# Layer 0's state space in chunks of four tokens, with one scan over 64 chunks

## The reference, cut to what matters

```
# S5_WIDTH 512 = 32 groups of 16 channels, 64 complex states per group, L = 256
def s5_mixer(u, lam_re, lam_im, log_dt, b_re, b_im, c_re, c_im, d_skip, w_glu, b_glu):
    uf = u.reshape(bsz, L, S5_GROUPS, S5_GROUP)
    lam_bar = exp(lam * dt)
    b_bar = ((lam_bar - 1.0) / lam)[..., None] * bmat
    bu = complex(einsum('gnp,blgp->blgn', b_bar.real, uf), einsum('gnp,blgp->blgn', b_bar.imag, uf))
    hstate[t] = lam_bar * hstate[t - 1] + bu[t]            # an associative scan over the 256 tokens
    y = (einsum('gpn,blgn->blgp', c_re, hstate.real) - einsum('gpn,blgn->blgp', c_im, hstate.imag)
         + d_skip * uf)
    y = gelu(y)
    return y * sigmoid(y @ w_glu + b_glu)
```

## Time and profile before

| | before |
|---|---|
| median of 3 runs | 1175.95 us (1174.27 to 1177.32) |
| the profiled execution, its own time | 1179.43 us |
| its span, first to last instruction | 1177.5 us |
| TensorE / VectorE / ScalarE / GpSimd busy | 1063.6 / 793.3 / 506.6 / 371.3 us |
| mean granted TensorE clock | 0.953 of full speed |
| VectorE's first instruction / GpSimd's first after its loads | at 7.9 / 21.9 us |
| end of layer 0's last product | about 296.6 us |

### The profile page before, as it was taken

How to read it: one execution, slowest core, us unless ns; L and a number is a source line. 1 busy time by engine, 2 the same in 40 slices (tenths; PEclk the granted TensorE clock), 3 DMA queues, 4 the chain that set the end, 5 groups by cost and what they waited for, 6 DMA issues and landing times.

```text
span 1177.5 us, 15099 instructions
## 1 busy us (share of the span) xinstructions
PE 1063.6 (90%) x5902; PEld 906.1 (77%) x5902; DVE 793.3 (67%) x1217; ACT 506.6 (43%) x692; POOL 371.3 (32%) x386
## 2 busy tenths in 40 slices
PE   6699898959789897899999997997999999999994
PEld 5466565638688687898888986886998888998883
DVE  5799999976776588444555767666544455767664
ACT  6244235323553343444554332443444555434452
POOL 3715365670372607073442675000000000320001
PEclk9799899888889898999999998998999999999997
DMA  7343232236765476577656664553666545563641
GB/s 257 95 121 94 72 106 91 90 117 206 225 206 171 128 230 210 179 236 217 192 145 210 210 203 143 180 182 104 181 183 192 167 119 160 168 174 110 211 162 54
DMA packets 95047, 191.36 MB, mean 163 GB/s; under 512 B 6800, under 2 KB 10128, under 8 KB 94976
## 3 DMA queue, kind: packets, MB, share of 16 engines
q1 hardware_dynamic: 87408, 166.81, 46.4%
q0 software_dynamic: 6416, 20.88, 5.9%
q10 hardware_dynamic: 1152, 2.71, 0.6%
HBM read 189.32 MB, written 1.05 MB: 162 GB/s over the span
## 4 chain that ended last, share of the span: by engine, by line
PE 67%; DVE 23%; ACT 3%; POOL 3%; issue 3%; DMA 1%; DVEq 0%; SPq 0%; POOLq 0%; ACTq 0%
PE G L557 12%; PE G L559 12%; PE G L558 12%; PE G L566 7%; PE G L569 6%; PE G L568 6%; DVE WL L1359 6%; DVE AR L1638 1%; ACT WH L989 1%; DVE AR L1640 1%; PE B L520 1%; DMA RAW<-in_even_w_in 1%; DVE AR L1621 1%; DVE AR L1620 1%; DVE AR L1459 1%
## 5 line engine op out<-in xcount | busy, mean ns | idle before, releaser
L1359 DVE TENSOR_TENSOR WL<-RAW,WH 128x1024 fp32r<-128x1024 f32 (+2 forms) x306 | 398.0, 1303 | 272.5 <-ACT WH L989 271.6
L989 ACT ACTIVATE WH<-RAW 128x1024 fp32r<-128x1024 f32 (+2 forms) x306 | 319.6, 1047 | 353.6 <-PE G L559 228.9
L557 PE MATMUL G<-WH,HTh 128*128 128x512 f32 (+2 forms) x624 | 257.5, 413 | 20.1 <-DVE WL L1359 19.9
L559 PE MATMUL G<-WL,HTh 128*128 128x512 f32 (+2 forms) x624 | 246.3, 395 | 0.0
L558 PE MATMUL G<-WH,HTl 128*128 128x512 f32 (+2 forms) x624 | 246.0, 394 | 0.0
L566 PE MATMUL G<-HTh,WH 128*128 128x256 f32 x736 | 213.1, 290 | 12.9 <-DVE WL L1359 7.5
L569 PE MATMUL G<-HTh,WL 128*128 128x256 f32 x736 | 211.2, 287 | 0.0
L568 PE MATMUL G<-HTl,WH 128*128 128x256 f32 x736 | 211.2, 287 | 0.0
L557 PEld LDWEIGHTS G<-WH,HTh 128*128 128x128 f32 x624 | 121.1, 194 | 52.8 <-issue 17.7
L566 PEld LDWEIGHTS G<-HTh,WH 128*128 128x128 f32 x736 | 144.3, 196 | 15.3 <-DVE WL L1359 9.3
L568 PEld LDWEIGHTS G<-HTl,WH 128*128 128x128 f32 x736 | 144.2, 196 | 0.1
(11 more groups left out here) (325 smaller groups left out, 1391.8 us busy)
## 6 DMA issues: line engine op xcount, KB each, us to landing
RAW<-in_w_in SPq DMA_DIRECT2D x176, 512.0 KB, 3.8
RAW<-in_even_w_in SPq DMA_DIRECT2D x40, 512.0 KB, 3.6
AR<-in_w_ada POOLq DMA_DIRECT2D x72, 256.0 KB, 3.3
RAW<-in_odd_w_in SPq DMA_DIRECT2D x16, 512.0 KB, 4.4
RAW<-in_w_proj_ret SPq DMA_DIRECT2D x16, 512.0 KB, 4.5
RAW<-in_w_out SPq DMA_DIRECT2D x16, 512.0 KB, 3.5
RAW<-in_even_w_out SPq DMA_DIRECT2D x12, 512.0 KB, 3.6
AR<-in_w_ada SPq DMA_DIRECT2D x24, 256.0 KB, 4.5
```

The source lines that it names most:

```text
L557: nc.tensor.matmul(o, xh, wh, start=begins, stop=False)
L559: ins = nc.tensor.matmul(o, xh, wl, start=False, stop=ends)
L989: return nc.scalar.activation(out_, ps, ACT.Copy, **kw)
L1359: vt(wl, raw, wh.bitcast(F32), ALU.subtract).then_inc(*dve.mark(LO, n))
```

## The change

The tokens of layer 0's state space are taken in chunks of four. Inside a chunk the output is one product with a matrix of 128 by 128 (`NEAR`, with the skip D in it); across chunks the state after each chunk is needed only, so that there are 64 positions to scan and not 256. The states' inputs are one product per tile over four tokens at once (`M2`, the matrix B times powers of lambda, 128 by 128), the outputs one product for four tokens (`M3`, C times powers of lambda). The input `u` is first laid out by chunk (`U4`).

These matrices are made on the chip at the start: powers of lambda and the products with C by VectorE (`s5_powers`, `s5_states_out`), the products with B by GpSimd (`s5_states_in`, six instructions 768 wide), their copies into block form by ScalarE (`s5_block`), `NEAR` by 33 small matmuls and ten copies, `M2` by 32 transposes and eight copies, `U4` by 16 copies. The tables are half as long and made by VectorE alone, in steps 17 to 21 and 25. The scan is two instructions, 1024 wide, over all 16 tiles at once, in steps 43 and 44. The gelu moves from step 87 to steps 60 to 66. The weight pieces and all other layers keep their order.

```diff
-AT_S5_IN = (20, 24, 28, 32, 36, 40, 44, 48, 52, 55, 59, 63, 67, 70, 73, 76)
-AT_S5_SCAN = (26, 30, 34, 38, 42, 46, 50, 54, 57, 61, 65, 69, 72, 75, 78, 82)
-AT_S5_OUT = (33, 37, 41, 45, 49, 53, 56, 60, 64, 68, 71, 74, 77, 81, 83, 84)
-AT_S5_H = (29,) + AT_S5_OUT[:15]
+AT_S5 = {"powers": 1, "factor": 5, "c": 7, "out_re": 9, "out_im": 13, "table": {17: 0, 18: 1, 19: 2, 20: 3, 21: 4, 25: 5},
+         "block": {2: "b0", 8: "cp", 11: "re", 14: "hre", 15: "im", 16: "him"}, "spread": (17, 18, 19, 20), "near": 21,
+         "near_out": (22, 23), "turn": (24, 25, 26, 27), "in": (29, 31, 37, 40), "scan": (43, 44),
+         "back": (45, 48, 51, 54), "out": (49, 52, 55, 58)}
...
-AT_GELU = 87
+AT_GELU = {"square": 60, "cube": 61, "tanh": 63, "y": 64, "hi": 65, "lo": 66}
...
+            def s5_near():
+                ps = take(("near",), S5_NEAR.of("k"))
+                pe.wait_ge(*S5_P.of("dd"))
+                nc.tensor.matmul(ps[:, :], IDENT[0:32, :], DD.rearrange("p a b -> p (a b)"), start=True, stop=False,
+                                 skip_group_check=True)
+                pe.wait_ge(*S5_BLOCK.of("him"))
+                for i in range(16):
+                    for r in range(2):
+                        ins = nc.tensor.matmul(ps[:, 32 * i:32 * i + 32], H[:, r, i, :], CP[:, r, i, :], start=False,
+                                               stop=i == 15 and r == 1, skip_group_check=True)
+                ins.then_inc(*told("near"))
+            def s5_turn(q):
+                for r in range(2):
+                    ps = take(("m2", q, r), S5_M2.of(q, r))
+                    for j in range(4):
+                        ins = nc.tensor.transpose(ps[:, 128 * j:128 * j + 128], H[:, r, 4 * q + j, :], IDENT)
+                    ins.then_inc(*told("m2", q, r))
+            def s5_in(q):
+                ps = take(("s5in", q), S5_IN.of("a2", q))
+                pe.wait_ge(*S5_U4.of("u"))
+                pe.wait_ge(*S5_M2.of(q, 1))
+                for r in range(2):
+                    for j in range(4):
+                        c = 256 * r + 64 * j
+                        ins = nc.tensor.matmul(ps[:, c:c + 64], M2[q][:, r, j, :], U4[:, 4 * q + j, :], start=True,
+                                               stop=True)
+                ins.then_inc(*told("s5in", q))
+            def s5_out(q):
+                ps = take(("s5y", q), S5_Y.of(q))
+                pe.wait_ge(*S5_NEAR.of("k"))
+                pe.wait_ge(*S5_H.of(q))
+                for j in range(4):
+                    o, i = ps[:, 64 * j:64 * j + 64], 4 * q + j
+                    nc.tensor.matmul(o, M3[:, 0, i, :], SH[:, q % 2, 0, j, :], start=True, stop=False)
+                    nc.tensor.matmul(o, M3[:, 1, i, :], SH[:, q % 2, 1, j, :], start=False, stop=False)
+                    ins = nc.tensor.matmul(o, NEAR[:, i, :], U4[:, i, :], start=False, stop=True)
+                ins.then_inc(*told("s5y", q))
...
+            def s5_block(what):
+                for r in range(2):
+                    for g in range(2):
+                        pr, k = slice(64 * g, 64 * g + 64), slice(16 * g, 16 * g + 16)
+                        h = H[pr, r, :, :].rearrange("p i (b k) -> p b i k", b=4)
+                        if what == "b0":
+                            act.wait_ge(l_br, 16)
+                            act.wait_ge(*S5_P.of("zero"))
+                            ins = copy(h[:, 0, :, k], BR[pr, r, :, :])
+                        elif what == "cp":
+                            act.wait_ge(*S5_V.of("cd"))
+                            ins = copy(CP[pr, r, :, k], CD[pr, r, :, :])
+                        elif r == (what in ("im", "him")):
+                            if what in ("hre", "him"):
+                                act.wait_ge(*S5_P.of(what[1:]))
+                                dense = (HA if what == "hre" else HD)[pr, :]
+                                ins = copy(h[:, 1:4, :, k], dense.rearrange("p (b i k) -> p b i k", b=3, i=16))
+                            else:
+                                act.wait_ge(*S5_V.of("zero"))
+                                act.wait_ge(*S5_V.of(what))
+                                o = M3[pr, r, :, :].rearrange("p i (t k) -> p t i k", t=4)
+                                dense = (OA_ if what == "re" else OC_)[pr, :]
+                                ins = copy(o[:, :, :, k], dense.rearrange("p (t i k) -> p t i k", t=4, i=16))
+                ins.then_inc(*act.mark(S5_BLOCK, what))
...
+            def s5_spread(b):
+                act.wait_ge(*GA.of("u", 1))
+                act.wait_ge(*S5_P.of("im"))
+                act.wait_ge(*S5_BLOCK.of("him"))
+                for q in range(4):
+                    u = UT[32 * q:32 * q + 32, :, :].rearrange("p j (c t) -> p j t c", t=4)
+                    ins = copy(U4[32 * b:32 * b + 32, 4 * q:4 * q + 4, :], u[:, :, 3 - b, :])
+                if b == 3:
+                    ins.then_inc(*act.mark(S5_U4, "u"))
...
+            def s5_y(q):
+                act.wait_ge(*side("s5y", q))
+                for tk in range(4):
+                    y = UT[32 * q:32 * q + 32, :, :].rearrange("p j (c t) -> p j t c", t=4)
+                    ps = bank_of["s5y", q][32 * tk:32 * tk + 32, 0:256].rearrange("p (j c) -> p j c", j=4)
+                    ins = copy(y[:, :, tk, :], ps)
...
+            def s5_states_out(part):
+                def product(o, r, p):
+                    c = CD[:, r].unsqueeze(1).to_broadcast([P, 4, 16, 16])
+                    l = LP[:, p, :, :].unsqueeze(3).to_broadcast([P, 4, 16, 16])
+                    vt(o.rearrange("p (t i k) -> p t i k", t=4, i=16), c, l, ALU.mult).then_inc(*dve.tick())
+                if part == "re":
+                    dve.wait_ge(*S5_V.of("cd"))
+                    product(OA_, 0, 0)
+                    product(OB_, 1, 1)
+                    dve.wait_ge(*dve.prev)
...
+                ps = bank_of["s5in", q][:, :].rearrange("p (r n) -> p r n", r=2)
+                tc, tsn = (flat(x[:, 4 * q:4 * q + 4, :]).unsqueeze(1).to_broadcast([P, 2, 256]) for x in (TC, TS))
+                vt(SA.rearrange("p (r n) -> p r n", r=2), ps, tc, ALU.mult).then_inc(*dve.mark(S5_IN, "a1", q))
+                vt(SB_.rearrange("p (r n) -> p r n", r=2), ps, tsn, ALU.mult).then_inc(*dve.mark(S5_IN, "a2", q))
+                c = slice(256 * q, 256 * q + 256)
+                dve.wait_ge(*S5_IN.of("a2", q))
+                vt(V[:, 0, c], SA[:, 0:256], SB_[:, 256:512], ALU.add).then_inc(*dve.mark(S5_IN, "c1", q))
+                vt(V[:, 1, c], SA[:, 256:512], SB_[:, 0:256], ALU.subtract).then_inc(*dve.mark(S5_IN, "c2", q))
+            def s5_scan(r):
+                dve.wait_ge(*S5_IN.of("c2", 3))
+                dve.wait_ge(*S5_P.of("decay"))
+                nc.vector.tensor_tensor_scan(V[:, r, :], flat(DECAY), V[:, r, :], 0.0, ALU.mult, ALU.add).then_inc(
+                    *dve.mark(S5_G, r))
...
+            def s5_states_in():
+                def product(o, r, p):
+                    b = BR[:, r].unsqueeze(1).to_broadcast([P, 3, 16, 16])
+                    l = LP[:, p, 0:3, :].unsqueeze(3).to_broadcast([P, 3, 16, 16])
+                    own()
+                    gtt(o.rearrange("p (d i k) -> p d i k", d=3, i=16), b, l, ALU.mult).then_inc(*pool.tick())
+                pool.wait_ge(l_br, 16)
+                pool.wait_ge(*S5_V.of("lp"))
+                product(HA, 0, 0)
+                product(HB, 1, 1)
                 own()
...
+                gtt(HA, HA, HB, ALU.subtract).then_inc(*pool.mark(S5_P, "re"))
+                product(HB, 0, 1)
+                product(HD, 1, 0)
                 own()
...
+                gtt(HD, HD, HB, ALU.add).then_inc(*pool.mark(S5_P, "im"))
...
+            def s5_back(q):
+                pool.wait_ge(*S5_G.of(1))
+                if q == 0:
+                    own()
+                    nc.gpsimd.memset(SASB.rearrange("p (a c) -> p a c", c=64)[:, :, 0:1], 0.0).then_inc(
+                        *pool.mark(S5_P, "sh"))
+                g = V[:, :, 256 * q:256 * q + 256]
+                tc, tsn = (flat(x[:, 4 * q:4 * q + 4, :]).unsqueeze(1).to_broadcast([P, 2, 256]) for x in (TC, TS))
                 own()
...
+                gtt(SA2.rearrange("p (r n) -> p r n", r=2), g, tc, ALU.mult).then_inc(*pool.tick())
                 own()
...
+                gtt(SB2.rearrange("p (r n) -> p r n", r=2), g, tsn, ALU.mult).then_inc(*pool.tick())
+                if q >= 2:
+                    pool.wait_ge(*side("s5y", q - 2))
+                a, b = (x.rearrange("p (r j c) -> p r j c", r=2, j=4)[:, :, :, 0:63] for x in (SA2, SB2))
+                o = SH[:, q % 2, :, :, 1:64]
                 own()
...
+                gtt(o[:, 0], a[:, 0], b[:, 1], ALU.subtract).then_inc(*pool.tick())
                 own()
...
+                gtt(o[:, 1], a[:, 1], b[:, 0], ALU.add).then_inc(*pool.mark(S5_H, q))
```

(28 more changed lines are left out.)

462 lines of the change are left out of this document (204 added, 258 removed).

## The result

The changed kernel takes 1143.59 us, the median of four runs (1141.15 to 1146.18), against 1176.45 us before (median of four, one more than ahead): a ratio of 0.9724 [0.9692, 0.9755], 32.9 us less. The forecast was 1130 us (1108 to 1150), 46 us less. The profiled execution's own time is 1145.8 us with a span of 1144.0.

A forecast was written before the change was run, and what follows sets the result against it. Layer 0 was taken as bound by VectorE up to step 84, the rest by TensorE. 41.2 - 2.7 + 7.5 = 46 us off the profiled 1179.4 gave 1133.4, for the median 1130 us (1108 to 1150).

The forecast's parts named there:

- steps 28 to 84: Layer 0, steps 28 to 84: TensorE becomes the bound, 129.6 us instead of 170.8, 41.2 us less.
- tail: Steps 85 to the end of layer 0: 39 us instead of 46.5, 7.5 less, the gelu being done by step 66.
- layers 1 to 3: After layer 0: instructions kept, nothing counted; another length than 883 us would be a sign of being wrong.
- its sign: Steps 28 to 84: TensorE busy over 0.95 at a clock near 1.00, VectorE below 0.8 and waiting mainly for `hi`.
- The wait at step 49: Step 49: `s5_out(0)` waits for the second scan and GpSimd's first back turn; states 3 us after TensorE asks.
- Steps 16 to 27: Layer 0 before step 28: other waits replace those for the tables; step 28 starts at 82 us, 2.7 us later.
- the rival of the longer start: Start of layer 0: GpSimd and VectorE hold each other up, step 28 at 95, 33 us gained, 1143 us; chance 0.20.
- 7.9 of `NEAR`: Steps 17 to 28: TensorE's work for `NEAR` priced at 7.9 us, within 29.5 us of TensorE work.
- the main case: Whole kernel: the prediction's own case, 1120 to 1140 us; chance 0.46.
- The floor: Rival: waits of steps 28 to 84 mostly vanish, start as before; 63 us gained, 1113 us; chance 0.17.
- order costs more: Rival: in-order waits between four engines keep 57 steps at 2.7 us instead of 2.3; gain 22, 1154 us; chance 0.10.
- the 1.9 from which they decide: Slower rival: ScalarE's 66 added copies at 1.9 us each add 48 us and the gain is gone; chance 0.04.

The follow-up runs named there:

- The load runs: Changed kernel plus useless VectorE products at 16 steps from 28 to 76: five each, ratio 0.9841 to the kernel before; ten each, 1.0124.
- the late gelu: Changed kernel with the state space's activation computed in steps 83 to 87 instead of 60 to 66; ratio 0.9745 to the kernel before.
- the run with all three edits: Changed kernel with small products in steps 21 to 24, preparation and turning back on VectorE; 1134.1 us, ratio 0.9633 to the kernel before.

## Why the prediction was right or wrong

Against the execution profiled (1133.4 forecast, 1145.8 measured) the terms are off by +14.8 (step 28), +3.5 (steps 28 to 84), -3.3 (tail) and -2.6 us (layers 1 to 3), together 12.4.

**Steps 28 to 84** were right in the mechanism: TensorE became the bound, 133.1 us against 129.6 forecast and 170.8 before, VectorE busy for 88.5 against 98.8 and idle mostly for `hi`. The load runs show that VectorE's relief did it. That the sum came so near is partly luck: TensorE's waits were 8.1 us and not 13, its work 125.0 and not 116.6, of which 6.8 are lost in two low stretches of 13.6 us together. So TensorE was busy for 0.94 of the stretch at a clock of 0.95, under what the forecast had named as its sign. The wait at step 49 was 3.2 us against 3. Not in the sum was what follows it: the clock is at 0.5 from 144 to 154 us, 5 us of work lost. A scan took 2.28 us against 2.56. A small product at full clock cost 0.22 us, as taken from the rows; the 60 cycles that the Trainium skill, "TensorE: Matmul & The Clock Gate", section "Back-to-back issue gap", gives for 1 to 64 columns are not met by 32 or 64 columns here: it is 0.11 us for each of the two records, some 260 cycles of 2.4 GHz, and each has a weight load of its own (PE and PEld both x6032).

**Steps 16 to 27** is the step that failed, "step 28 starts at 82, 2.7 us later": 96.8, and 94.6 in a second execution, the size that the rival of the longer start had. Of the 14.8 us, 10.2 are there at step 20 already (53.5 forecast, 63.7 measured). Two things were mis-sized and one was not seen, and the runs part them.
- "GpSimd ends its powers at 38.0 and starts six instructions of 768 columns [...] 2.1 each." The powers ended at 44.7, since VectorE's new 1024-column instructions stand beside them. The six products took 12.5 us together, as forecast (12.6), but by luck: the first three took 2.27, 2.36 and 2.69, the others 1.5 to 1.8, and 2.1 came from rows that were held up by VectorE themselves. That GpSimd's went on "undelayed" in the earlier trace rows was a wrong reading as far as the rows tell: 768 columns took 1.50 us with no VectorE instruction beside them, so 1024 would take 2.0 by an estimate in proportion, and 2.70 is more. I had named a collision and given it 0.20, but at the six products; it came at the powers before them, and at the head norm behind them, which took 7.8 us and not the 5.0 of the earlier trace rows. Taking GpSimd's part away brought step 28 5.5 us forward; changing its order brought nothing to be told apart.
- "7.9 of `NEAR`": 12.4 for the products, and one or two steps behind them at half clock too. Priced at full clock by a row of full clock, although the stretch was known to run at 0.80. I had put the low clock down to the stall before; it followed the products.
- ScalarE's waits. Its copies were dearer than "0.49 is the nearest row" (on 32 partitions, 256 columns took 0.66 us, 512 columns 0.59), but its work from 58.3 to 96.8 us was 28.8 us, and 28 were forecast. What the forecast did not have is that ScalarE stands still for 7.5 us of this stretch, for the small products. It is the bound that shows when either of the others is lifted, and why 12 us at step 24 became 4.6 at step 28.

These don't add: TensorE, ScalarE and the VectorE-GpSimd pair are within some us of each other from step 16 to 27. With GpSimd's part moved and the small products spread, step 28 came at 88.0, 6 us behind the forecast and behind a wait for ScalarE; what would be left with ScalarE's copies lifted too was not tried.

**The tail** took 35.7 us against 39 and holds no wait for the gelu, as forecast; the late gelu gives 7.8 of it back. The early gelu costs 3.4 us in steps 60 to 84, for which the forecast had 5.

**Layers 1 to 3** took 880.2 us where a length other than 883 was a sign of being wrong. No run was made on these 2.6 us; TensorE's waits there are 1.2 us less and its low stretches 1.8 us shorter.

**The rivals.** The result is not in the 1120 to 1140 of the main case; it is the 1143 of the longer start, given 0.20. That number is met closer than its mechanism: it had step 28 at 95 from GpSimd waiting before each of its six products and from copies at 0.8, and nothing of the clock under the small products. The floor and "order costs more" did not come, ScalarE's copies took 0.43 to 1.06 us and not the 1.9 from which they decide, and no transfer held the kernel: 230 GB/s in the tail.

## What to carry to other kernels

Before moving work to GpSimd, look at what VectorE does at that time: in both directions an instruction beside a long one of the other engine took up to that one's whole length more, so small operations took up to eight times as long, and with the six products on VectorE the kernel took 8 us less. A product's price depends on the clock of its stretch, and that clock was halved by a block of small products and around waits of 3 us and more. The small products did no such harm among large ones. Where three engines are close, remove one cost and read which wait ends last then, before pricing the next.

## What the runs showed of the hardware

- VectorE's 8-column operation at 56.04 us ended at 57.42, with GpSimd's 1.81 us product (to 57.39); GpSimd's 16-column ones took 1.07 beside VectorE's 1.2. Both engines can be the loser, other than the earlier trace rows was read. The Trainium skill, "SBUF — State Buffer", section "SBUF: two separate sides", says that of a GpSimd instruction and a VectorE one in a two-port mode or with two inputs in SBUF, whichever starts first keeps the shared pair of ports for the whole instruction; these rows agree, as far as they show, since the mode of the one at 56.04, which has one tensor input, is not in the profile.
- The clock of a stretch with TensorE busy throughout fell to 0.5 some 2 to 5 us after 32 products of 32 columns began, at either place, and did not when they stood in eights between 512-column ones.
- Waits of 3.2, 2.9 and 5.6 us (step 49 of the changed kernel, the turns with the small products spread, the turns without them) went with 7 to 10 us at 0.5 that began at most 2 us before or 0.5 us behind their end; this is 3.4 to 5 us of work lost on top of the wait. The length varies: 3.4 us at 0.5 behind the wait of 2.9 in the run with all three edits, 17.1 with the wait of 5.3 at step 51; and in the wait of 6.0 us for the late gelu the 0.5 began 0.5 us after the wait did and lasted 10.2 us. Where the wait at step 49 was taken away, so was its low stretch.
